# Expert tiles of 32 rows in a two-layer mixer and mixture-of-experts trunk, turned by VectorE

## What is computed

```python
def grouped_moe(h, router_w, router_b, w_gate, w_up, w_down):
    ...
    expert_idx = best_group[:, None] * EXPERTS_PER_GROUP + top_idx      # 2 of 16 experts for each token
    ...
    gates = jnp.sum(jax.nn.one_hot(expert_idx, N_EXPERTS, dtype=jnp.float32) * w[..., None], axis=1).astype(h.dtype)
    out = jnp.zeros_like(h)
    for e in range(N_EXPERTS):
        a = jax.nn.silu(h @ w_gate[e]) * (h @ w_up[e])                  # 1024 -> 512
        out = out + gates[:, e:e + 1] * (a @ w_down[e])                 # 512 -> 1024
    return out
```

## Time and profile before

| what | us |
| --- | --- |
| median of 3 runs (lowest, highest) | 1120.03 (1118.56, 1121.53) |
| the profiled execution, its own time | 1120.89 |
| its span, first to last instruction | 1119.3 |
| expert tiles of layer 0, PE from the first L1216 to the last L1234 | 364.04 to 646.9 |
| expert tiles of layer 1, the same | 839.01 to 1087.0 |
| TensorE busy (share of the span) | 969.8 (87%) |
| VectorE, ScalarE, GpSimd busy | 308.2, 226.0, 102.5 |
| moved by DMA | 334.64 MB, 299 GB/s over the span |

### The profile page before, as it was taken

One profiled execution on the slowest core, in us unless ns is written; L12 is line 12 of the kernel. 1 busy time (PEld: TensorE's weight loads), 2 busy tenths in 40 slices (PEclk: granted clock), 3 DMA queues, 4 the chain that ended last, 5 costly groups with the idle time before them and its releaser, 6 DMA issues.

```text
span 1119.3 us, 16030 instructions
## 1 busy us (share of the span) xinstructions
PE 969.8 (87%) x5879; PEld 575.6 (51%) x5880; DVE 308.2 (28%) x695; ACT 226.0 (20%) x432; POOL 102.5 (9%) x174
## 2 busy tenths in 40 slices
PE   3799999999986999999999929999959988877980
PEld 2247434566446555555555516877445544544540
DVE  1104101864253111111111145357241111111113
ACT  2210102343020122122222223034021211111211
POOL 2000101004202200000000130000010000000002
PEclk9899999999995999999999969999959999999995
DMA  9977778549949698799999954646178999999973
GB/s 343 353 284 277 283 268 360 213 166 336 242 160 355 218 384 325 301 395 385 395 375 388 387 196 142 225 197 236 76 259 313 365 387 402 397 392 404 391 271 112
DMA packets 90564, 334.64 MB, mean 299 GB/s; under 512 B 9312, under 2 KB 23280, under 8 KB 74000
## 3 DMA queue, kind: packets, MB, share of 16 engines
q1 hardware_dynamic: 74112, 289.77, 67.9%
q0 software_dynamic: 10016, 33.89, 10.1%
q10 hardware_dynamic: 6400, 10.49, 2.7%
HBM read 307.84 MB, written 28.74 MB: 301 GB/s over the span
## 4 chain that ended last, share of the span: by engine, by line
PE 45%; DMA 18%; DVE 4%; issue 1%; ACT 1%; POOL 0%; ACTq 0%; SPq 0%; POOLq 0%; DVEq 0%
PE bank L1216 18%; DMA weight_ring<-in_w_up_dram 9%; PE bank L1234 9%; DMA weight_ring<-in_w_gate_dram 8%; PE bank L1014 3%; PE bank L1130 2%; PE bank L1017 2%; PE bank L1200 2%; PE bank L1261 2%; PE bank L1225 1%; PE bank L1092 1%; PE bank L1065 1%; DMA weight_ring<-y_by_expert,slot_numbers 1%; PE bank L1077 1%; PE bank L970 0%
## 5 line engine op out<-in xcount | busy, mean ns | idle before, releaser
L1216 PE MATMUL bank<-weight_ring,qk_tokens 128*64 128x256 f32 x2560 | 304.9, 391 | 32.6 <-DMA weight_ring<-in_w_up_dram 29.6
L1216 PEld LDWEIGHTS bank<-weight_ring,qk_tokens 128*64 128x64 f32 x2560 | 193.1, 141 | 139.8 <-issue 64.6
L1234 PE MATMUL bank<-weight_ring,qk_tokens 128*64 128x512 f32 x640 | 152.9, 598 | 0.0
L1622 DVE TENSOR_TENSOR qk_tokens<-qk_tokens,bank 64x256 f32<-64x256 f32 x80 | 33.8, 423 | 328.7 <-ACT qk_tokens L904 328.7
L1014 PE MATMUL bank<-weight_ring 128*128 128x256 f32 (+1 forms) x320 | 97.8, 464 | 4.9 <-ACT weight_ring L795 3.1
L1017 PE MATMUL bank<-weight_ring 128*128 128x512 f32 (+1 forms) x256 | 84.9, 489 | 0.0
L1130 PE MATMUL bank<-weight_ring 128*128 128x512 f32 x192 | 83.4, 594 | 1.4 <-ACT weight_ring L864 1.4
L1014 PEld LDWEIGHTS bank<-weight_ring 128*128 128x128 f32 x320 | 61.8, 196 | 40.3 <-issue 34.8
L904 ACT ACTIVATE qk_tokens<-bank 64x256 f32<-64x256 f32 x80 | 30.1, 376 | 206.2 <-PE bank L1216 205.9
L1234 PEld LDWEIGHTS bank<-weight_ring,qk_tokens 128*64 128x64 f32 x640 | 42.4, 136 | 54.2 <-issue 45.7
L904 ACT ACT_TABLE_LOAD x40 | 51.3, 1283 | 85.1 <-issue 74.9
(11 more groups left out here) (173 smaller groups left out, 731.4 us busy)
## 6 DMA issues: line engine op xcount, KB each, us to landing
weight_ring<-in_w_gate_dram SPq DMA_DIRECT2D x64, 1024.0 KB, 9.0
weight_ring<-in_w_up_dram SPq DMA_DIRECT2D x64, 1024.0 KB, 8.9
weight_ring<-in_w_down_dram SPq DMA_DIRECT2D x64, 1024.0 KB, 9.5
weight_ring<-in_w_mod_dram SPq DMA_DIRECT2D x24, 2048.0 KB, 8.1
weight_ring<-in_w_in_dram SPq DMA_DIRECT2D x12, 1024.0 KB, 10.0
qk_tokens<-h_by_expert POOLq DMA_DIRECT2D x40, 256.0 KB, 7.2
y_by_expert<-qk_tokens ACTq DMA_DIRECT2D x80, 128.0 KB, 7.0
weight_ring<-in_w_out_dram SPq DMA_DIRECT2D x4, 2048.0 KB, 11.7
```

Of the source, the lines that this page charges most:

```text
L1216: mm = pe.matmul(pb[hf][64 * r:64 * r + 64, 0:256], hTe[:, k, :], w[:, k, hf * 256:(hf + 1) * 256], start=(k == 0), stop=(k == KD - 1), ti ...
L1234: mm = pe.matmul(pb[4][64 * r:64 * r + 64, :], aTe[:, k, :], wdown(n)[:, k, r * 512:(r + 1) * 512], start=(k == 0), stop=(k == KF - 1), ti ...
L1622: V.tensor_tensor(ae[:, hf * 256:(hf + 1) * 256], sg[:, hf * 256:(hf + 1) * 256], pb[hf][SLOTS:P, 0:256], ALU.mult).then_inc(s_a[l], 1)
```

## The change

- `SLOTS` is 32. Layer 0 gives each expert two tiles at least (`LEAST`), layer 1 one; the total is rounded up to an even number. With the counts above there are 40 tiles in layer 0 and 22 in layer 1.
- The stationary operand of gate, up and down is 128x32, four side by side; a tile has 32 gate and up matmuls and 16 down matmuls, all with 256 moving columns. The transposes on TensorE are gone: VectorE transposes 32x32 blocks, of the rows (`turn_rows`, 128x256) and of the activations (`turn_a`, two of 64x128).
- Row block b of the transposed operands holds the model rows that are 8 apart (down: 4 apart), so each partition's weights are read from HBM as eight (down: four) neighbouring rows; the down parts' runs are 8 KB and not 4 KB.
- In layer 0 the down products of a tile are done after gate and up of the next (`LEAST[l] == 2`); in layer 1 right after its own. The loops over the experts are written out 16 times.
- The rows of the first four tiles (`AHEAD`) are picked by one product with 128 slots for each token tile, eight matmuls with 512 moving columns in layer 0 and four in layer 1, and turned out of PSUM by VectorE, four 32x256 transposes a tile. Later tiles' rows come from HBM, two buffers, four transfers of 32 KB a tile (packets of 1 KB where they were of 4 KB). Results leave through two buffers, four stores of 32 KB a tile (packets of 1 KB, before 2 KB).
- `h_by_expert` is zeroed by 17 writes of 512 KB from 128 partitions; the end of `y_by_expert` by 9 more of the same size in the same place, where before it was copied from zeroed rows during the tiles (L705).
- `load_small` waits for the scatter, and not for the first row load.

```diff
-SLOTS = 64
+SLOTS = 32
...
-    NTILE = 2 * NALL * P // SLOTS + NE
+    NTILE = 2 * NALL * P // SLOTS + 2 * NE + 4
+    AHEAD = P // SLOTS
+    Q = D // AHEAD
...
+    NZ = NTILE * SLOTS // P
     NT = [NALL if l < DEPTH - 1 else NX for l in range(DEPTH)]
+    LEAST = [2 if n == NALL else 1 for n in NT]
...
-        ae = qkbuf[0:SLOTS, 2048:2560]
-        aTe = qkbuf[:, 2560:2816].rearrange("p (k s) -> p k s", k=KF)
-        ysb = qkbuf[:, 2816:3328]
-
-        picked = qkbuf[:, 2560:2816].rearrange("p (t s) -> p t s", t=NALL)
-        same = qkbuf[:, 2816:3328].rearrange("p (k t s) -> p k t s", k=2, t=NALL)
+        hrow = [qkbuf[:, (4 + i) * Q:(5 + i) * Q] for i in range(2)]
+        hTe = qkbuf[:, 6 * Q:7 * Q]
+        sg = qkbuf[2 * SLOTS:P, 7 * Q:8 * Q]
+        ae = qkbuf[0:2 * SLOTS, 7 * Q:8 * Q]
+        ysb = [qkbuf[:, (8 + i) * Q:(9 + i) * Q] for i in range(2)]
+        aTe = qkbuf[:, 2 * Q:2 * Q + P]
+        picked = qkbuf[:, 0:2 * Q].rearrange("p (t s) -> p t s", t=NALL)
...
-                    rows_ = slice(hf * k // 2 * P, (hf + 1) * k // 2 * P)
-                    order = "(k p) n -> p k n" if k == KF else "(p k) n -> p k n"
-                    src = (w[l, e, rows_, :].rearrange(order, p=P) if isinstance(e, int)
-                           else w[l, bass.ds(e, 1), rows_, :].rearrange("a " + order.replace("-> p k", "-> p (a k)"), p=P))
+                    part = slice(hf * k // 2, (hf + 1) * k // 2)
+                    if k == KD:
+                        src = (w[l, e].rearrange("(p k) n -> p k n", p=P)[:, part, :] if isinstance(e, int)
+                               else w[l, bass.ds(e, 1)].rearrange("a (p k) n -> p a k n", p=P)[:, 0, part, :])
...
-                        sp.wait_ge(s_gu[l], first * 2)
+                        sp.wait_ge(s_gu[l], first)
...
-                    sp.wait_ge(s_hTp[l], 1)
-                    sp.wait_ge(s_hrow[l], 16)
+                    sp.wait_ge(s_first.sem, s_first.at(l, 1))
+                    sp.wait_ge(s_scat.sem, s_scat.at(l, 32 * NT[l]))
...
-                    for n in range(NTILE):
-                        pool.dma_start(hsort[n * SLOTS:(n + 1) * SLOTS, :], zeros).then_inc(s_hz, 16)
+                    for n in range(NZ):
+                        pool.dma_start(hsort[n * P:(n + 1) * P, :], zeros).then_inc(s_hz, 16)
+                    for n in range(2 * NE * SLOTS // P, NZ):
+                        pool.dma_start(ysort[n * P:(n + 1) * P, :], zeros).then_inc(s_yz, 16)
...
                 pool.wait_ge(s_scat.sem, s_scat.at(l, 32 * NT[l]))
...
-                with pool.Fori(1, total) as T:
-                    pool.wait_ge(s_hTp[l], T + 1)
-                    pool.dma_start(hrow, hsort[bass.ds((T + 1) * SLOTS, SLOTS), :]).then_inc(s_hrow[l], 16)
+                pool.wait_ge(s_tot.sem, s_tot.at(l, 1))
+                pairs = pool.value_load(tab[l][0:1, NE + 1:NE + 2], min_val=LEAST[l] * NE // 2 - 2, max_val=NTILE // 2 - 4)
+                with pool.Fori(0, pairs) as n:
+                    for i in range(2):
+                        pool.wait_ge(s_hT[l], n * 2 + (3 + i))
+                        for q in range(AHEAD):
+                            pool.dma_start(hrow[i][q * SLOTS:(q + 1) * SLOTS, :],
+                                           hsort[bass.ds((n * 2 + (AHEAD + i)) * SLOTS, SLOTS), q * Q:(q + 1) * Q]).then_inc(s_hrow[i][l], 16)
...
+                act.wait_ge(s_yz, 16 * (NZ - 2 * NE * SLOTS // P))
...
+                def silu(T):
+                    act.wait_ge(s_gu[l], T + 1)
+                    nc.scalar.activation(sg, pb[0][0:2 * SLOTS, 0:Q], ACT.Silu).then_inc(s_si[l], 1)
...
+                def store_rows(T, i, stored):
+
                     act.wait_ge(s_d[l], T + 1)
-                    act.wait_ge(s_yd[l], T * 32 + 32)
-                    nc.scalar.copy(ysb, pb[4][:, :]).then_inc(s_y[l], 1)
+                    if stored is not None:
+                        act.wait_ge(s_yd[i][l], stored * 64)
+                    nc.scalar.copy(ysb[i], pb[4][:, 0:Q]).then_inc(s_y[l], 1)
                     act.wait_ge(s_y[l], T + 2)
-                    for hf in range(2):
-                        act.dma_start(ysort[bass.ds(T * SLOTS, SLOTS), hf * 512:(hf + 1) * 512],
-                                      ysb[hf * SLOTS:(hf + 1) * SLOTS, :]).then_inc(s_yd[l], 16)
+                    tile_rows = slice(T * SLOTS, (T + 1) * SLOTS) if isinstance(T, int) else bass.ds(T * SLOTS, SLOTS)
+                    for q in range(AHEAD):
+                        act.dma_start(ysort[tile_rows, q * Q:(q + 1) * Q], ysb[i][q * SLOTS:(q + 1) * SLOTS, :]).then_inc(s_yd[i][l], 16)
...
+                with act.Fori(0, pairs) as n:
+                    for i in range(2):
+                        silu(n * 2 + (4 + i))
+                        store_rows(n * 2 + (3 + i), 1 - i, n + (1 + i))
+                store_rows(pairs * 2 + 3, 1, pairs + 1)
...
-                def model_rows(rows_, k):
...
+                def gate_up(T, n, use, first):
+
+                    pe.wait_ge(s_hT[l], T + 1)
+                    if LEAST[l] == 2 and not isinstance(T, int):
+                        pe.wait_ge(s_a[l], T)
                     for k in range(KD):
+                        if first and k % HK == 0:
+                            arrived(n, 2 * (k // HK), use)
+                            arrived(n, 2 * (k // HK) + 1, use)
+                        for g in range(4):
+                            w, f = (wgate(n), wup(n))[g // 2], (g % 2) * P
+                            mm = pe.matmul(pb[0][32 * g:32 * g + 32, 0:Q].rearrange("p (c f) -> p c f", c=2), hTe[:, k * SLOTS:(k + 1) * SLOTS],
+                                           w[:, k, :].rearrange("p (c f) -> p c f", c=2)[:, :, f:f + P], start=(k == 0), stop=(k == KD - 1), tile_position=(0, 32 * g))
+                    mm.then_inc(s_gu[l], 1)
...
+                def down(T, n, use, first):
+
+                    pe.wait_ge(s_aT[l], T + 1)
                     pe.wait_ge(s_y[l], T + 1)
+                    for k in range(KF):
+                        if first and k % 2 == 0:
+                            arrived(n, 4 + k // 2, use)
+                        for g in range(4):
+                            mm = pe.matmul(pb[4][32 * g:32 * g + 32, 0:Q], aTe[:, k * SLOTS:(k + 1) * SLOTS],
+                                           wdown(n)[:, k, g * Q:(g + 1) * Q], start=(k == 0), stop=(k == KF - 1), tile_position=(0, 32 * g))
                     mm.then_inc(s_d[l], 1)
...
+                def later_tiles(lo, hi, n, use):
+                    with pe.Fori(lo + 1, hi) as T:
+                        gate_up(T, n, use, False)
+                        down(T - 1, n, use, True)
...
+                for t in range(NT[l]):
+                    pe.wait_ge(s_pick.sem, s_pick.at(l, t + 1))
+                    for hf in range(2):
+                        mm = pe.matmul(pb[6 + hf][:, :], picked[:, t, :], h2[:, t, hf * MH:(hf + 1) * MH], start=(t == 0), stop=(t == NT[l] - 1))
+                mm.then_inc(s_first.sem, 1)
+                if LEAST[l] == 2:
+                    gate_up(0, l, 1, True)
+                    later_tiles(0, hi, l, 1)
+                    for e in range(1, NE):
+                        lo = hi
+                        gate_up(lo, l + e, e // RING + 1, True)
+                        hi = first_tile_index(e + 1)
+                        down(lo - 1, l + e - 1, (e - 1) // RING + 1, False)
+                        later_tiles(lo, hi, l + e, e // RING + 1)
+                    down(hi - 1, NE - 1 + l, (NE - 1) // RING + 1, False)
+                else:
+                    lo = 0
+                    for e in range(NE):
+                        with pe.Fori(lo, hi) as T:
+                            gate_up(T, l + e, e // RING + 1, True)
+                            down(T, l + e, e // RING + 1, True)
+                        lo = hi
...
+                def first_rows(T):
+
+                    for q in range(AHEAD):
+                        rows_ = pb[6 + q // 2][T * SLOTS:(T + 1) * SLOTS, (q % 2) * Q:(q % 2 + 1) * Q]
+                        ins = V.transpose(hTe[q * SLOTS:(q + 1) * SLOTS, :].rearrange("p (b s) -> p b s", b=KD), in_blocks(rows_, KD))
+                    ins.then_inc(s_hT[l], 1)
+
+                def turn_rows(i, loaded):
+
+                    dve.wait_ge(s_hrow[i][l], loaded * 64)
+                    V.transpose(hTe.rearrange("p (b s) -> p b s", b=KD), in_blocks(hrow[i], KD)).then_inc(s_hT[l], 1)
+
+                def product(T):
+                    dve.wait_ge(s_si[l], T + 1)
+                    if not isinstance(T, int) or T > 0:
+                        dve.wait_ge(s_aT[l], T)
+                    V.tensor_tensor(ae, sg, pb[0][2 * SLOTS:P, 0:Q], ALU.mult).then_inc(s_a[l], 1)
+                    dve.wait_ge(s_a[l], T + 1)
+
+                def turn_a():
+                    for c in range(2):
```

(10 more changed lines are left out.)

188 lines of the change are left out of this document (70 added, 118 removed).

## The result

The changed kernel takes **1078.7 us** (median of 4 runs, 1075.5 to 1079.9) against 1120.0 beside it: 0.963 of the time before, 95% interval 0.960 to 0.965, a gain of 41 us. Forecast were 1103.5 and a gain of 16.5. The profiled execution took 1075.5, its span is 1073.7 where before has 1119.3; it was the shortest of the four, 3.2 us under their median.

A forecast was written before the change was run, and what follows sets the result against it. The weight stream, through a tile's price on the DMA engines, was taken as the bound. Gains of 11.6 us (layer 0) and 9.5 (layer 1) less 4.6 given back made 16.5, so 1103.5 us; range 1078 to 1130.

The forecast's parts named there:

- The bound and what decides: Tile phases: a faster tile meets the weight stream in layer 0 at once; a tile's DMA price decides, not TensorE.
- that price: What a 32-row tile costs the weight stream: 1.7 us, between 1.2 (bytes) and 2.45 (packets).
- price by packets: Tiles' stores: 181 ns a packet at 1 KB, 1.45 us a tile; with 0.9 by bytes, 1.2 was taken.
- "bytes": Rival for the tile's price on the stream: 1.2 us a tile, 1076 us; bytes or less had chance 0.20.
- The rule on ports: Tiles' stores: 64 partitions on one side reach 8 of 16 ports, half rate; 32 fare no worse.
- Start of layer 0: Layer 0 before the stream: pick 9.1 us, first gate and up at 359, expert 3's load at 374.5.
- VectorE's transposes: Turning of rows and activations in the tiles: 0.3 us each, a layer 1 tile of 7.0 us.
- Row chain: Row loads and stores: 5.8 us a tile, under the stream's pace; as a rival, longer than the stream, chance 0.05.
- Layer 1: Layer 1's tiles: last part at 1069.5, end at 1077.5 instead of 1087.0, 9.5 us gained.
- Give-backs: Ends of both layers: later last stores 2.6 us, their slower landing in layer 0 2 us, 4.6 us lost together.
- Zero writes and 8 KB runs: Zero writes, 13.6 MB, stay hidden under the output projection; the down weights' 8 KB runs bring nothing.
- bytes or less: Case for the whole kernel's time: tile price by bytes or lower, 1070 to 1087 us, chance 0.20.

The follow-up runs named there:

- e17: The kernel before, a tile's rows read from expert 0's gate weights as one plain transfer of 128 partitions x 2 KB: 1110.7 us (0.992).
- e1: The changed kernel with the down weights loaded the old way, two runs of 4 KB instead of one of 8 KB: 1083.8 us (0.970).
- e8: The changed kernel with each tile's four row loads written as one transfer and its four stores as one: 1168.0 us (1.042).
- e5: The kernel before, its row load landing in 128 partitions in one nested transfer instead of in 64: 1307.0 us (1.168).
- e13: The changed kernel, rows read from expert 0's gate weights as one plain transfer of 128 partitions instead of four of 32: 1078.8 us (0.963).
- e6: The kernel before, its row load cut into two of 2 KB packets, still into the same 64 partitions: 1118.4 us (0.999).
- e15: The changed kernel with layer 1's loop in layer 0's order, next gate and up before this tile's down products: 1076.1 us (0.960).
- e16: The changed kernel itself, as yardstick beside e15 on the same chip: 1080.8 us (0.965).

## Why the prediction was wrong, step by step

**The bound and what decides: right.** TensorE's tile went to 5.2 to 5.6 us at full clock (3.45 to 3.61 and 1.73 to 1.98), the stream took over in layer 0 at once, and the price of a tile on the DMA engines set the time.

**The step that failed is that price.** The prediction split the 2.45 us of a 64-row tile so: 0.62 us "is then the row load, 1.8 us the stores", because the hole in the earlier trace rows stood 2 us after the stores were issued. But the row load was in flight then too, issued at 966.6 and landed at 973.3, and the stores' data came after the hole. Rightly split it is 1.16 for the crossing of the row load (e17), and 1.29 for the rest, which by bytes would be about 0.65 each for rows and stores (not measured apart). From the wrong split the prediction drew a price by packets (225 ns for 2 KB, 181 for 1 KB) that the halved tile would keep. In its terms the 1.7 were stores 1.2, rows 0.37, and 0.13 of queue overhead for which it had no row. Measured: stores 0.40, rows 0.44 by themselves and 0.29 for their crossing, which was 1.16 before. Half of 1.16 is 0.58 by the bytes; that it is halved once more, when the four loads land in turn all over the partitions, fits crossed ports and is argued only. 1.13 instead of 1.7. In layer 0 that is 36 x 0.57 = 20.5 us, the whole of the difference at its end (615.8 for 635.4). The rival "bytes" (1.2 us a tile, 1076 us) was right in the size of the price and not in what makes it up. That its 1076 lies so near 1078.7 is partly luck: some 7 us of layer 1 that the price would have given did not come, and neither did the give-backs. The rule on ports, which the prediction held against the stores, belonged to the row loads. The packets were not as the prediction counted them either: a tile's rows are booked as 64 packets of 2 KB, not 128 of 1 KB.

**Start of layer 0: right.** Pick 8.8 us (forecast 9.1), first gate and up at 356.8 (359, with the 1.9 us that were there already), expert 3's load at 374.7 (374.5). Inside, it was made up otherwise: VectorE's four turns out of PSUM take 1.8 us between one tile and the next, and the second gate and up ran 5.38 us, not 3.5 (granted clock 0.68 there, behind 2.5 us of waiting for VectorE).

**VectorE's transposes: too small.** 0.3 us each were taken, 0.65 for rows and 2 x 0.41 for the activations were measured. Layer 0 hides them; in layer 1 a tile takes 7.54 us at full clock, not 7.0, and the last eleven 8.2 on average.

**Row chain: right.** Row loads land in 5.5 us at the median, VectorE never waits for them.

**Layer 1: right sign, other bound.** The first loads of experts 3 and 15 stand 193.8 us apart, and 12 x 14.9 and 14 tiles at 1.13 would be 194.6. So the cheap tile gave its part here too; but with eleven tiles in the last five experts TensorE was late from 953 on, and of the 11 us that the price would have given beyond the forecast, 4 arrived. TensorE's clock has a part in that which the prediction's sum for layer 1 leaves out: from the gate and up at 953.31 to that at 1035.12 stand ten tiles, 8.2 us each, with the clock granted at 0.89; some of their gate and up took 4.54 us where others took 3.50. Against 7.54 that is 6 to 7 us.

**Give-backs: wrong.** 4.6 us were forecast, none came. The last store of layer 0 lands in 1.46 us (2.26 before), not up to 7, and from the last down product to the gather it is 4.4 us as before (4.6). The four issues cost 0.48 us each, but the last tile is now half as much to copy out and store.

**Zero writes and 8 KB runs: right.** The output projection takes 41.47 us as before, and the last of the writes has landed by 310, long before the scatter; the runs brought nothing (e1).

**Chances.** The time lies just inside the range, at its lower edge (1078.0), in the case "bytes or less" that had 0.20. The range was cut by bounds for the sum of rows and stores; it would have been wider had the split itself been doubted.

## What to carry to other kernels

A hole in the transfer rate belongs to the transfer whose data move in it: put issue and landing of every transfer in flight beside the hole before giving it to one of them. A small load that is spread over 32 or 64 partitions beside a full stream slows that stream down as long as it lands (its packets take 57 to 65 ns per KB instead of 39), and a plain one to 128 partitions hardly does (39 to 41); a nested pattern with 2 or 4 in its slowest dimension is far worse than separate transfers (1168 us for 1079 here, e8). When a stage is bound by a stream, count what is issued per stage: one tile less for each of eleven experts was worth 24 us, over half of it at the ends. And where TensorE comes to wait between tiles, its tile is not to be priced at full clock alone: here it was 8.2 us for 7.5.

## What had not been expected of the hardware

A nested row load of 256 KB landed in 17.4 us where a flat one takes 7 (e5), a nested store of 128 KB in up to 27 us (e8). On GpSimd's queue the trace books packets longer than the runs of the code: two runs of 1 KB as 2 KB in the change, four as 4 KB in e13, two of 2 KB as 4 KB in e6. Stores from 64 partitions do not slow the packets of a load beside them as loads to 64 do (39 ns per KB in the kernel before, the same as alone); they only take their own time. And the same kernel stood at 0.963, 0.965 and 0.967 of before on three occasions, so of differences under half a per cent only e15 beside e16 on one chip is told as one.
